# Two transformer blocks on one core: weight chunks converted at other points of ScalarE's order, two narrow roots with their first guess in PSUM, and a sum of squares placed inside a tile

## What is computed

```python
h = rms_norm(x, norm_mix_pre);  proj = h @ w_in
o_gla = gla_mixer(...)                      # gated linear attention, its output times silu(r)
o_nsa = nsa_mixer(...)                      # compressed, selected and windowed attention
mixed = sigmoid(merge_gla) * (o_gla @ w_proj_gla) + sigmoid(merge_nsa) * (o_nsa @ w_proj_nsa)
x = x + rms_norm(mixed @ w_out, norm_mix_post)
h = rms_norm(x, norm_ffn_pre)
f = (silu(h @ w_ffn_gate) * (h @ w_ffn_up)) @ w_ffn_down
x = x + rms_norm(f, norm_ffn_post)
# second block: h = rms_norm(x), z = h @ w_in_2, convolution and neighbourhood attention, then
x = x + mix @ w_out_2
h = rms_norm(x, norm2_g_2)
x = x + (silu(h @ w_gate_2) * (h @ w_up_2)) @ w_down_2
```

## Time and profile before

| what | value |
|---|---|
| median of three runs | 1553.95 us (1551.8 to 1554.38) |
| profiled execution | 1554.4 us, its span 1552.4 us |
| PE matmuls busy | 1506.3 us, 97% of the span |
| DVE, ACT, POOL busy | 659.7, 586.3, 653.6 us |
| mean granted clock of PE | 0.986 |

### The profile page before, as it was taken

One profiled execution on the slowest core, in us unless ns is written; L12 is line 12 of the kernel. 1 busy time (PEld: TensorE's weight loads), 2 busy tenths in 40 slices (PEclk: granted clock), 3 DMA queues, 4 the chain that ended last, 5 costly groups with the idle time before them and its releaser, 6 DMA issues.

```text
span 1552.4 us, 20374 instructions
## 1 busy us (share of the span) xinstructions
PE 1506.3 (97%) x7376; PEld 1192.7 (77%) x7376; DVE 659.7 (42%) x1095; ACT 586.3 (38%) x914; POOL 653.6 (42%) x302
## 2 busy tenths in 40 slices
PE   7999999999999988999999998999999999999998
PEld 6888788666668876888888885777667888888887
DVE  5212444775543456333331006777736433333001
ACT  4131332655462334222332224566654322232221
POOL 3433312663234433444445442665324444444443
PEclk9999999999999989999999998999999999999999
DMA  4522211111113322333333332421112333333333
GB/s 168 170 82 68 81 54 41 42 54 43 55 55 95 95 70 80 95 95 96 100 101 96 109 109 88 129 68 55 54 50 86 95 95 95 96 97 102 102 105 109
DMA packets 40893, 135.04 MB, mean 87 GB/s; under 512 B 4464, under 2 KB 8816, under 8 KB 40576
## 3 DMA queue, kind: packets, MB, share of 16 engines
q1 hardware_dynamic: 39504, 130.56, 28.1%
q10 hardware_dynamic: 1328, 3.64, 0.7%
HBM read 132.09 MB, written 2.10 MB: 86 GB/s over the span
## 4 chain that ended last, share of the span: by engine, by line
PE 70%; issue 19%; DVE 4%; POOL 4%; ACT 2%; DMA 0%; POOLq 0%; DVEq 0%; SPq 0%; ACTq 0%
PE bank L1033 18%; PE bank L1035 18%; PE bank L1034 18%; POOL wL L423 4%; PE bank L1062 2%; PE bank L1064 2%; PE bank L1063 2%; PE bank L1332 1%; PE bank L1333 1%; PE bank L1334 1%; DVE bank L1971 1%; PE bank L1202 1%; PE bank L1236 1%; PE bank L1197 1%; ACT wH L512 1%
## 5 line engine op out<-in xcount | busy, mean ns | idle before, releaser
L423 POOL TENSOR_TENSOR wL<-raw,wH 128x1024 fp32r<-128x1024 f32 x235 | 573.5, 2441 | 843.7 <-ACT wH L512 663.6
L512 ACT ACTIVATE wH<-raw 128x1024 fp32r<-128x1024 f32 x209 | 221.3, 1059 | 639.1 <-PE bank L1035 585.9
L1033 PE MATMUL bank<-aH,wH 128*128 128x512 f32 x1024 | 406.2, 397 | 13.6 <-POOL wL L423 7.5
L1035 PE MATMUL bank<-aH,wL 128*128 128x512 f32 x1024 | 400.8, 391 | 0.0
L1034 PE MATMUL bank<-aL,wH 128*128 128x512 f32 x1024 | 400.6, 391 | 0.0
L1033 PEld LDWEIGHTS bank<-aH,wH 128*128 128x128 f32 x1024 | 193.6, 189 | 64.4 <-issue 16.0
L1034 PEld LDWEIGHTS bank<-aL,wH 128*128 128x128 f32 x1024 | 193.7, 189 | 41.3 <-issue 2.0
L1035 PEld LDWEIGHTS bank<-aH,wL 128*128 128x128 f32 x1024 | 193.4, 189 | 40.6
L1033 PE MATMUL bank<-fH,wH 128*128 128x512 f32 x352 | 137.3, 390 | 0.0
L1034 PE MATMUL bank<-fL,wH 128*128 128x512 f32 x352 | 137.0, 389 | 0.0
L1035 PE MATMUL bank<-fH,wL 128*128 128x512 f32 x352 | 137.0, 389 | 0.0
(11 more groups left out here) (275 smaller groups left out, 1850.7 us busy)
## 6 DMA issues: line engine op xcount, KB each, us to landing
raw<-in_w SPq DMA_DIRECT2D x235, 512.0 KB, 3.5
bmk<-in_bias SPq DMA_DIRECT2D x6, 512.0 KB, 4.8
pj<-in_x SPq DMA_DIRECT2D x4, 512.0 KB, 6.5
out_x<-z2T SPq DMA_DIRECT2D x8, 256.0 KB, 3.5
ct<-in_ct ACTq DMA_DIRECT2D x3, 384.0 KB, 3.1
w1k<-in_w1k ACTq DMA_DIRECT2D x1, 1024.0 KB, 5.9
w1v<-in_w1v ACTq DMA_DIRECT2D x1, 1024.0 KB, 5.2
pv<-in_pv ACTq DMA_DIRECT2D x1, 128.5 KB, 4.6
```

Source lines behind the costliest of these rows:

```text
L423: pool.tensor_tensor(wL[:, c_slot, :], raw[:, c_slot, :], wH[:, c_slot, :].bitcast(F32), ALU.subtract).then_inc(sem("w_lo"), 1)
L512: act.activation(wH[:, s, :], raw[:, s, :], ACT.Copy).then_inc(sem("w_hi"), 1)
L1033: pe.matmul(bank[:], hi, H[:, ka, :], start=(k == 0), stop=False)
L1035: mm = pe.matmul(bank[:], lo, H[:, ka, :], start=False, stop=(k == p.k - 1))
```

## The change

It has three kinds of edit.

1. `ahead` stands at other places of ACT's order. At `pg` the first `ahead` goes in front of the large sigmoid, which becomes a `mid` step behind tile 0. In `gu1` chunk 4 is converted after the second square, not after the eighth; chunk 5 before the wide root; the table load is written out; and iteration 1 is unrolled, so that chunks 6 and 7 are converted between the steps of iteration 0. Before `gu2` one `ahead` moves in front of squares 2 and 3 (it stood between them), another in front of square 7.
2. Roots 2 and 4: ACT's Exp writes its guess to four columns of `B[5]` instead of to `root`. DVE's three steps take it from there, in another order: guess times x, times -0.5 times guess, plus 1.5 times guess. Root 6 keeps its guess in `root`, with the new order.
3. `total` of `gu1` goes behind k = 3 of tile 4 instead of ahead of tile 4. At `out2`'s end DVE makes the last `aL` before it adds the last square.

```diff
@@ -529,8 +529,8 @@
                                 square(sums * KD + t, lambda: B[(p.t0 + t) % NBANK][:], it)
                             ahead(p, base * p.nc4 // 4 + q, it, last)
                             q += 1
-                        if mid is not None and t == 1:
-                            mid()
+                        if mid is not None and t < 2:
+                            mid[t]()
                         if evict is not None:
                             evict(it, base + t)
                 n4 = p.nt // 4
@@ -556,12 +556,12 @@
                     act.wait_ge(sem("sq_used"), it * 4 + (n - 1))
                 act.activation(sq[:, n % 2, :], src(), ACT.Square).then_inc(sem("sq_ready"), 1)
 
-            def rsqrt(n, bank, width, summed, r=nr[:]):
+            def rsqrt(n, bank, width, summed, r=nr[:], guess=None):
 
                 act.wait_ge(*summed)
                 act.activation(r, bank, ACT.Ln, scale=1.0 / width, bias=vec("eps")).then_inc(sem("ln_ready"), 1)
                 act.wait_ge(sem("ln_ready"), n)
-                act.activation(r, r, ACT.Exp, scale=-0.5).then_inc(sem("nr_ready"), 1)
+                act.activation(r if guess is None else guess, r, ACT.Exp, scale=-0.5).then_inc(sem("nr_ready"), 1)
 
             def high_of_x(use, gain, ready=None, norm=None, beside=False, kts=range(KD)):
 
@@ -761,14 +761,12 @@
                 act.wait_ge(sem("bank_free"), NBANK + PH["mgn"].t0 + tiles)
                 act.activation(dst, dst, ACT.Sigmoid).then_inc(sem("gates_mix"), 1)
 
-            gate(sg, KD)
-
             def gate_and_split():
                 gate(sgn, 2 * KD)
                 act.wait_ge(sem("nsa_out"), NR)
                 for kt in range(KD // 2):
                     act.activation(onH[:, kt, :], pj[:, NQ + kt, :], ACT.Copy).then_inc(sem("on_hi"), 1)
-            gemm(PH["pg"], mid=gate_and_split)
+            gemm(PH["pg"], mid=(lambda: gate(sg, KD), gate_and_split))
 
             def high_mix(it, t):
                 act.wait_ge(sem("pn_mix"), it * 4 + (t + 1))
@@ -778,13 +776,15 @@
 
             act.preload_act_table_set("natural_log_exp_and_others")
             gemm(PH["out1"], sums=1)
-            rsqrt(2, narrow(B[4]), D, (sem("sum_ready"), 2), root)
+            rsqrt(2, narrow(B[4]), D, (sem("sum_ready"), 2), root, narrow(B[5]))
             high_of_x("h2", "g_ffn_pre", "res1", None, kts=range(0, 5))
             ahead(PH["gu1"], 0)
             high_of_x("h2", "g_ffn_pre", "res1", None, kts=range(5, KD))
             ahead(PH["gu1"], 1)
             for kt in range(KD):
                 square(2 * KD + kt, lambda: xT[:, kt, :])
+                if kt == 1:
+                    ahead(PH["gu1"], 2)
 
             def swiglu(p, tag, norm, by_k=False):
                 def silu(it, j):
@@ -797,12 +797,21 @@
                         .then_inc(sem(tag + "_fH"), 1)
 
                 if by_k:
-                    ahead(p, 2)
+                    ahead(p, 3)
                     rsqrt(*norm)
-                    ahead(p, 3)
+                    act.preload_act_table_set("silu_and_others")
+                    ahead(p, 0, 1)
                     silu(0, 0)
                     high_f(0, 0)
                     silu(0, 1)
+                    ahead(p, 1, 1)
+                    high_f(0, 1)
+                    silu(1, 0)
+                    high_f(1, 0)
+                    ahead(p, 2, 1)
+                    silu(1, 1)
+                    ahead(p, 3, 1)
+                    high_f(1, 1)
                 else:
                     ahead(p, 0)
                     ahead(p, 1)
@@ -812,8 +821,8 @@
                     high_f(0, 0)
                     silu(0, 1)
                     ahead(p, 3)
-                high_f(0, 1)
-                with act.Fori(1, p.nt // 4) as it:
+                    high_f(0, 1)
+                with act.Fori(2 if by_k else 1, p.nt // 4) as it:
                     for j in range(2):
                         ahead(p, 2 * j, it)
                         silu(it, j)
@@ -823,7 +832,7 @@
             swiglu(PH["gu1"], "ff1", (3, B[5][:], D, (sem("sum_ready"), 3)), True)
             act.preload_act_table_set("natural_log_exp_and_others")
             gemm(PH["dn1"], sums=3)
-            rsqrt(4, narrow(B[4]), D, (sem("sum_ready"), 4), root)
+            rsqrt(4, narrow(B[4]), D, (sem("sum_ready"), 4), root, narrow(B[5]))
 
 
             high_of_x("h3", "g_norm1", "res2", 4, True)
@@ -978,15 +987,17 @@
                     act.wait_ge(sem("out2_conv"), 1)
                 act.activation(aH[:, (t + 4) % KD, :], xT[:, t, :], ACT.Copy, scale=vec("g_norm2", t)).then_inc(sem("h4_hi"), 1)
 
-            for t in range(3):
+            for t in range(2):
                 square_and_high(t)
             ahead(q, 4)
-            square_and_high(3)
+            for t in range(2, 4):
+                square_and_high(t)
             ahead(q, 5)
             ahead(q, 6)
-            for t in range(4, KD):
+            for t in range(4, KD - 1):
                 square_and_high(t)
             ahead(q, 7)
+            square_and_high(KD - 1)
             swiglu(PH["gu2"], "ff2", (7, B[4][:], D, (sem("sum_ready"), 8)))
             p = PH["dn2"]
 
@@ -1312,9 +1323,9 @@
                     mm = pe.matmul(B[gu1_bank(t)][:], wH[:, s, blocks_[t]], aL[:, k, :], start=False, stop=(k == KD - 1))
                 if k % 2:
                     mm.then_inc(sem("chunk_done"), 1)
-            total(3 * KD, B[5])
             for t in range(4, 8):
-                tile_products(p, 0, t, 1, aH, aL, alone=B[gu1_bank(t)], idle=t < 6)
+                tile_products(p, 0, t, 1, aH, aL, alone=B[gu1_bank(t)], idle=t < 6,
+                              after=(lambda k: total(3 * KD, B[5]) if k == 3 else None) if t == 4 else None)
             with pe.Fori(2, p.nt // 4) as it:
                 tile_products(p, it, 0, 4, aH, aL)
             gemm(PH["dn1"], fH, fL, first=("ff1_fL", 2))
@@ -1571,14 +1582,14 @@
                 link(dve.tensor_scalar(nx[:], bank[:], 1.0 / D, EPS, ALU.mult, ALU.add))
                 newton(n)
 
-            def token_root(n, bank, width):
+            def token_root(n, bank, width, guess=root):
 
                 dve.wait_ge(sem("ln_ready"), n)
                 link(dve.tensor_scalar(root_x, narrow(bank), 1.0 / width, EPS, ALU.mult, ALU.add))
                 dve.wait_ge(sem("nr_ready"), n)
-                link(dve.scalar_tensor_tensor(root_t, root, -0.5, root, ALU.mult, ALU.mult))
-                link(dve.tensor_tensor(root_t, root_t, root_x, ALU.mult))
-                dve.scalar_tensor_tensor(root, root_t, 1.5, root, ALU.add, ALU.mult).then_inc(sem("root_ready"), 1)
+                link(dve.tensor_tensor(root_t, guess, root_x, ALU.mult))
+                link(dve.scalar_tensor_tensor(root_t, root_t, -0.5, guess, ALU.mult, ALU.mult))
+                dve.scalar_tensor_tensor(root, root_t, 1.5, guess, ALU.add, ALU.mult).then_inc(sem("root_ready"), 1)
 
             def low_of_x(use, gain, kt):
 
@@ -1885,7 +1896,7 @@
                         low_of_x(use, next_gain, kt - 1)
                 low_of_x(use, next_gain, KD - 1)
 
-            token_root(2, B[4], D)
+            token_root(2, B[4], D, narrow(B[5]))
             residual_and_low(zT, "g_mix_post", "res1", "h2", "g_ffn_pre", 1)
             clear_sum(2)
             for kt in range(KD):
@@ -1923,7 +1934,7 @@
             swiglu(p, "ff1", 2)
             clear_sum(3)
             copy_and_square(PH["dn1"], z2T, 3)
-            token_root(4, B[4], D)
+            token_root(4, B[4], D, narrow(B[5]))
             residual_and_low(z2T, "g_ffn_post", "res2", "h3", "g_norm1", 2)
             dve.wait_ge(sem("res2"), KD)
             dve.sem_inc(sem("ffn1_done"), 1)
@@ -2127,8 +2138,8 @@
                 add_square(5 * KD + 4 + t)
                 low_of_out(t)
             add_attended(KD - 1)
+            low_of_out(KD - 1)
             add_square(5 * KD + 4 + KD - 1)
-            low_of_out(KD - 1)
             norm(7, B[4])
             swiglu(PH["gu2"], "ff2")
             p = PH["dn2"]
```

## The result

Measured: **1539.26 us** (four runs, 1538.89 to 1541.13) beside 1552.88 us (four runs, 1551.8 to 1554.38) for the kernel before; the ratio is 0.9915 [0.9903, 0.9927]. Later sets of the same two kernels gave 1540.85 beside 1553.72 and 1540.61 beside 1553.81, inside the range. Over all runs of the two, 16 of the changed kernel and 74 of the kernel before, the medians are 1540.4 and 1553.9, so the change is worth 13.5 us where −12.0 was forecast. The profiled execution took 1538.92 us, its span 1536.9; between the two profiled executions stand 15.5 us.

The account below looks back on a forecast made before the run. PE, busy 1506.3 of 1552.4 us, was taken as the bound, so only its idle or slow-clock time pays. −0.6 − 2.9 − 6.0 − 0.87 − 1.9 + 0.3 = −12.0 gave 1542.2 us, range 1539.8 to 1546.5.

Parts of the forecast that it names:

- rival D: At the first hand-over the clock falls less, worth 2.4 us more: 1539.8; chance 0.10.
- Start of `pg`, −0.6: Converting before the table load and sigmoid removes 0.45 us idle and a slower restart before tile 2: −0.6 us.
- Roots 2 and 4, −2.9: With the guess in PSUM, a DVE root step falls from 1.63 to 0.16 us, twice: −2.9 us.
- `gu1`, −6.0: Earlier chunk conversions and the later sum start tile 8 at 616.95 instead of 623.0: −6.0 us, including 1.6 of clock.
- The stall of 0.2 at tile 8: In gu1, chunk 8 is ready at 616.9 but wanted at 616.75, so PE stalls 0.2 us.
- just in time, 0.3 to spare: In gu1, DVE's adds end at 595.6, before the sum of squares at 595.9 inside tile 4.
- 1.71 us case: Before gu2 the clock stayed up after 1.71 us idle; so tile 6's 0.95 idle keeps it up, saving 1.6.
- Before `gu2`, −0.87 −1.9 +0.3: Two earlier conversions remove PE's waits, −0.87 and −1.9 us; POOL's subtraction over `low_of_out(7)` costs 0.3.
- B: Bank waits and blocked DVE steps replace the stall and the clock falls again, costing 2.5 to 5: about 1546; chance 0.20.
- C: The root steps get no faster, as the 1.63 could be a wait for ACT's write: 1545.3; chance 0.06.
- F: The moves change nothing since ACT gets to them no earlier; only the roots gain, −2.9: 1551.3; chance 0.03.
- E: Slower: gu1's loop becomes DVE-bound, 1560.4 if DVE falls behind 1 us per remaining pair; chance 0.03.

Follow-up runs that it names:

- guess_in_sbuf: The changed kernel with Exp's guess for roots 2 and 4 written to free SBUF columns instead of PSUM; 1542.34 us, ratio 0.9933 to the kernel before.
- tile6_and_chunk8: The changed kernel with tile 6 of gu1 in bank 4 and chunk 8 converted before the silu and high copy of pair (1, 0); 1537.32 us, ratio 0.9893.
- tile6_bank: The changed kernel with tile 6 of gu1 in bank 4, which is free by then; 1540.67 us, ratio 0.9917 to the kernel before.
- the parts alone: Four kernels, each the kernel before plus one part of the diff: roots 1549.29 us, gu1 1546.61, gu2 1549.24, pg 1551.33.

## Why the prediction came out as it did

**What failed.** The mechanisms came out as worked out; sizes did not. In the sum, the term of the roots was mis-sized: −2.9, measured −3.55, since it left out the clock at PE's transposes. The cost of 0.3 before `gu2` was not there. Outside the sum, the clock in the code that nobody edited was put at nothing, and with it the range: its lower end was rival D's 1539.8, while `in2` alone, the same code, took 203.2 us in some executions of the changed kernel and 206.2 in another.

**Start of `pg`, −0.6.** Right: 12.62 became 12.03 (11.98 to 12.03 in five traces), and another 0.13 went in the step behind. The sigmoid's later end cost nothing.

**Roots 2 and 4, −2.9: the term that was mis-sized.** Measured −1.96 and −1.59 in after, −3.55 together. The two waits of PE account for 1.50 and 1.51 of it, close to the 1.47 each that was worked out. The mechanism, one SBUF input in place of two, is shown by guess_in_sbuf. What the sum left out is that an earlier end of the steps also moves PE's transposes. At root 2 they take 0.65 us for 1.11, because they now run before the granted clock halves. Windows of PE, first before, then after (the transposes stand at 565.33 and 563.63):

```profile
564.00:570.00 6.00, 2.31 (x7) 0.50 0.29 87
```

```profile
560.00:564.00 4.00, 2.78 (x22) 1.00 0.42 131
```

Rival D asked whether the clock falls less here. It still stands at 0.50 from 566 to 572, so D isn't what happened, but its idea, that less idle time saves clock too, holds for 0.46 us. At root 4 they take 1.11 in after and 0.65 in tile6_and_chunk8, with the same code around them: in after they start at 934.00, and the window 934 to 944 has 0.50; in tile6_and_chunk8 they start at 932.24, and the clock is at 1.00 up to 933.

**`gu1`, −6.0.** Measured −5.7 between the two profiled executions. Tile 4 begins 24.46 after `gu1`'s start for 27.26 (−2.80; worked out −2.87). Tile 6 begins 13.07 after tile 4 (worked out 12.7) after 0.79 us for the third eviction (0.95). Tile 8 follows 11.01 later (11.05). The stall of 0.2 at tile 8 isn't in the list of waits; tile6_bank shows that it is latent, since with tile 6 begun 1 us earlier tile 8 waits 0.85. The sum "just in time, 0.3 to spare" came 0.2 late: the twelfth matmul's turn ends at 591.11 + 2.72 = 593.83, the last add at 594.00, the sum starts at 594.05. The prediction named a wait for the sum inside tile 4 as a sign of being wrong; it is there, at 0.2 us, too short for the list of waits, and the argument stands. Of the 5.7, the 1.6 of half clock was lost in two of the four traces of the kernel before; beside the other two, whose way from `gu1`'s first product to tile 8 is 53.0 and 53.1 us for after's 48.5, the change is worth 4.5 and 4.6 here. The forecast counted the 1.6 as certain. Nor did its 1.71 us case show that the clock stays up: the window 1187 to 1189 of the earlier trace rows ends before the matmul at 1189.03 that it was to speak of (up to 1191 the clock did stay at 1.00), and the same wait was followed by half clock in two other traces. In after's own case, 0.79 us of wait, the clock stayed up in all five traces.

**Before `gu2`, −0.87 −1.9 +0.3.** The gains are −1.04 and −1.90. The cost was not there: `low_of_out(7)` began at 1171.91, close to the end of POOL's subtraction (1169.40 + 2.86 = 1172.26), took 0.90 in place of 0.75, and no wait of PE follows it. So the net is −2.9 for −2.5.

**The sum.** −0.7 − 3.55 − 5.7 − 2.9 = −12.9 for −12.0. From the median of all runs of before, 1553.9, that gives 1541.0, 0.6 from the changed kernel's 1540.4. The rest of the distance in the first measurement, 1.1 us from 1540.4 to 1539.26, is which executions it happened to take. Of the 15.5 us between the two profiled executions 3.0 lie in `in2`, and single times of the kernel before run from 1548.8 to 1555.6 us. The forecast's own range had no term for this. So the miss itself, 0.54 us beyond the range, is luck of one set; the 0.9 us by which the sum is short is not.

**The rivals.** B (banks and held DVE steps in the stall's place) was there in kind, not in size: 0.79 at tile 6, a product of 1.70, an add held, and no fall of the clock. C and F are out by guess_in_sbuf and by the parts alone. E, `gu1` bound by DVE, is out: from tile 8 to the end of `dn1` every trace takes 315.5 to 315.7 us.

**What stays open.** The changed kernel has the lowest value of `in2` in four of five traces, the kernel before in none of four. The spans say that this overstates it: those four traces have spans of 1536.6 to 1537.1 us, the fifth 1538.9, and of all 16 executions 7 are under 1538 and 9 over it. Whether its timing favours the low value isn't settled, and what sets the clock in a given execution there was not tried. One fall can be placed. In before the clock halves near 997 us with PE busy for 9.31 of the 10 us ahead of it and idle for no more than 0.41 us at a time; but 1.95 us of the busy time are 16 matmuls of two columns each (timeline of PE, then windows, before):

```profile
994.69 1.95 PE L1343 MATMUL bank<-ct,sq 128*128 128x2 f32 x16 [0.41 <-ACT sq L846]
```

```profile
987.00:997.00 10.00, 9.31 (x48) 1.00 0.27 94
997.00:1001.00 4.00, 4.00 (x12) 0.57 0.44 131
```

In after the same matmuls are followed by 1.00 (window 987 to 991). Why the one execution loses the clock there and the other doesn't, no run here tells.

## What to carry to other kernels

When an engine's order puts a wait ahead of work that another engine needs, moving the awaited work later moves that need too. The same `total` edit made the kernel 4.1 us slower alone, and took 2.4 us off the way to tile 8 behind a reordered ACT, so price each edit with everything queued behind its wait. A tiny VectorE step in a hand-over is worth giving a PSUM input when GpSimd subtracts over it: two hand-overs gave 3.55 us. When a stall is removed, look for the next one within a microsecond of it and move both together; tile 6's bank gave nothing alone. And when an effect is of the size of the clock's scatter, compare traces step by step between the same matmuls, and give the range a term for the steps that nothing touches.

## What the runs showed of the hardware that was not expected

- The same 3.25 us of idle time of PE, in the same code, was followed by a granted clock of 0.50 in some executions and 1.00 in others; in both cases PE was busy for the whole window from 612 to 615. The difference is 1.6 us a time, 12.60 against 10.98.
- The clock also halved with hardly any idle time ahead of it: near 997 us in before, behind 0.41 us of wait and 16 matmuls of two columns (rows above).
- ACT's Exp of four columns took 0.18 us with PSUM as its destination and 0.21 with SBUF. The Trainium skill (ScalarE: Activation LUTs, Step-by-step: what each stage is for) calls PSUM the lower-latency port for ACT's results; these rows agree, by 0.03 us (0.18 against 0.20 at root 4).
- The hold between POOL and DVE goes both ways: in after, POOL's subtraction begun at 1169.40, inside DVE's `low_of_out(6)`, took 2.86 us, where 2.40 is usual; the 0.46 more is less than the 0.60 us that the two overlapped:

```profile
1169.26 0.74 DVE L2127 SCALAR_TENSOR_TENSOR aL<-xT,pv,aH 128x512 fp32r<-128x512 f32 x1
```
